# Values in fp32 on halves of the array's columns, distance table in fp32r

## The chip, the cores and the metric

One Trainium2 chip, one of its cores. The metric is the device time of one execution in microseconds (us), smaller is better. Before the change three runs took 2018.55 to 2023.57 us, with a median of 2019.44 us.

## The reference

Two transformer blocks on 512 frames with a width of 1024. The first has two attentions of eight heads of 64: one causal with a forgetting term (the "fox" heads), one in chunks with a table of biases by distance. The second adds 16 meta tokens in front and has an attention in a window of chunks with a sink (eight heads, keys and values shared by four), beside a gated linear attention. Around them stand projections, branch matrices, feed-forward parts and norms. The lines that the change touches, with softmax probabilities `p` that multiply values, and the table's bias:

```python
# first block, causal attention (q_block of 128 rows)
p = jax.nn.softmax(logits, axis=-1).astype(v.dtype)
return jnp.einsum('bhqk,bkhd->bqhd', p, v)
# first block, chunked attention
bias = rel_table[:, rel].astype(jnp.float32)
logits = jnp.einsum('bcqhd,bckhd->bchqk', qc, kb).astype(jnp.float32) * scale
logits = logits + bias[None, None]
p = jax.nn.softmax(logits, axis=-1).astype(v.dtype)
out = jnp.einsum('bchqk,bckhd->bcqhd', p, vb)
# second block, window attention
of = (jnp.einsum('bkgcqm,bmkd->bcqkgd', p[..., :N_META], vm)
      + jnp.einsum('bkgcqs,bcskd->bcqkgd', p[..., N_META:N_META + NB], vb))
```

## The kernel before

All is fp32 in and out. A large product is made of three matmuls in fp32r, a form of fp32 that is rounded: rounded times rounded, rounded times rest, rest times rounded. For that each weight and activation is split into a `_hi` tile (ScalarE, ACT, copies and rounds) and a `_lo` tile (VectorE, DVE, subtracts). Weights come in chunks of 1 MB into `W_raw`, and each chunk is split on ACT and DVE before its 48 matmuls.

The first attention stage (`front_steps`, with 64 units of 128 query rows of one head: eight fox heads, then eight chunked heads) is woven by a written table into the projections (`front_project`): in each step TensorE (PE) does nine to eleven projection matmuls and one unit's part. A unit goes this way. PE computes the scores of two heads at once in a PSUM bank each (`front_scores`, the two heads in the upper and lower 64 rows of the array), and adds the bias: for the chunked heads a plain fp32 matmul of the reversing matrix `exch` with the table `BAND`. DVE takes the maximum, ACT the exponential (tile `PR`), DVE the sum's inverse and the scaling. Two steps later PE turns the probabilities (L816) into the bank `TURNED`, ACT copies them out rounded (`PT_hi`), and DVE subtracts for the rest (`PT_lo`, L1962). After every fourth unit stands a phase (`front_values`): two heads, two blocks of 128 queries, the probabilities times the values. The stationary operand is `VHL`, a head's values rounded and their rest side by side, 128 columns; `PT_hi` and `PT_lo` stream through it one after the other. So the sum lies in two halves of the partitions of bank `PVOUT`, which ACT copies out (`OSIDE`) and DVE adds (`OSUM`, L1970); from two phases ACT and DVE make `O_hi` and `O_lo`. PE's queue waits before the next phase until DVE has added (`f_sum`), and before each turning until `PT_lo` of the unit before is done (`f_lo`).

The second attention stage (`win_steps`, 32 units) is woven in the same way into other projections. Its values are `VW`, its probabilities `PTW_hi`, `PTW_lo` for the window's keys and `PTM_hi`, `PTM_lo` for the 16 meta keys (`win_output`); the sums are `OSIDE2`, `OSUM2`, and the semaphores `att_lo`, `att_sum`.

The 24 MB of the conditioning matrix `wada` are mostly multiplied on DVE (L2584), three instructions for a part of the steps of the first stage. In the same stage DVE prepares the table (`band_bias`, L2006).

Of the kernel before, what the change touches and what calls it, by code (L numbers as in the profile page):

```python
# [9 lines left out]
FP32 = mybir.dt.float32  # L10
F32R = mybir.dt.float32r
# [5 lines left out]
P = 128  # L17
D = 1024
# [140 lines left out]
def build_program(nc, wts, wfg, wlow, wdown, wada, cond, vecs, xT, metaT, gate_w, band_rel, cf, cb, cw, cs, out):  # L159
    st, words = plan()  # L160
    n_chunks = len(words)
    with ExitStack() as ctx:
# [16 lines left out]
        with ExitStack() as over:  # L179
            PT_hi = sb("PT_hi", [P, 2, NB, 2 * P], F32R, over)  # L180
            PT_lo = sb("PT_lo", [P, 2, NB, 2 * P], F32R, over)
# [21 lines left out]
        OSIDE, OSUM = T[:, 2 * D:2 * D + SEQ], T[:, 2 * D + SEQ:2 * D + 2 * SEQ]  # L203
        OSIDE2, OSUM2 = T[:, 4 * TOK:4 * TOK + SEQ], T[:, 4 * TOK + SEQ:4 * TOK + 2 * SEQ]
# [15 lines left out]
        with ExitStack() as over:  # L220
            QH, QL, KH, KR, VHL = [], [], [], [], []
            for g in range(2):
# [4 lines left out]
                VHL.append(sb(f"VHL{g}", [P, NB, 4, P], F32R, over))  # L227
# [41 lines left out]
        with ExitStack() as over:  # L269
# [4 lines left out]
            VW = sb("VW", [P, NB + 1, 2, P], F32R, over)  # L274
            PTW_hi = sb("PTW_hi", [P, 2, SEQ], F32R, over)
            PTW_lo = sb("PTW_lo", [P, 2, SEQ], F32R, over)
            PTM_hi = sb("PTM_hi", [META, 2, 2 * P], F32R, over)
            PTM_lo = sb("PTM_lo", [META, 2, 2 * P], F32R, over)
# [378 lines left out]
        def _(pe):  # L657
# [95 lines left out]
            def front_scores(t):  # L753
# [13 lines left out]
                for o, n, _, _, _, _ in pair:  # L767
                    if fox:
                        last = mm(o[:, i * P:w], ident_b, causal_b, start=False, stop=True, skip_group_check=True)
                    else:  # L770
                        h = n - HEADS
# [2053 lines left out]
```

## Time and profile before

| | |
|---|---|
| median of three runs | 2019.44 us |
| the profiled execution | 2021.3 us |
| its span, first to last instruction | 2019.5 us |
| PE busy | 1956.0 us, 97% |
| DVE busy | 1023.5 us, 51% |
| ACT busy | 716.8 us, 35% |
| matmul records, weight loads | 10879 each |
| first attention stage | about 80 to 318 us |
| second attention stage | about 1296 to 1412 us |

How to read it: PE's row counts matmuls, PEld its weight loads, which run beside them. A matmul's shown length includes its way through the array, and the next one starts before it ends, so the distance between two starts tells what one costs. A plain fp32 matmul stands in the trace as two records, an fp32r matmul as one. The shape before the sizes is rows * columns of the stationary operand.

### The profile page before, as it was taken

Reading aid. Unit: us, or ns where it says so; the run is one execution under the profiler, and the core shown is the slowest. Engines: PE = TensorE matmul, PEld = TensorE weight load, DVE = VectorE, ACT = ScalarE, POOL = GpSimd, SP = SyncE. Lnnn points to the kernel's source line nnn. Section 1 sums busy time; section 2 is a strip of 40 time slices with the busy share of each in tenths; the row PEclk is TensorE's granted clock in tenths of the full one; section 3 lists DMA queues with packets and bytes.
Section 4 is the critical chain, followed back from the end, with each engine's and each line's share of the span. In section 5 each row is a group of like instructions: output and inputs, shape, how many; then the busy total and the mean of one; then the engine's idle time right before and its main releaser. Section 6 shows DMA issues by size and latency. Waiting matters only on the chain.

```text
span 2019.5 us, 26744 instructions
## 1 busy us (share of the span) xinstructions
PE 1956.0 (97%) x10879; PEld 1648.6 (82%) x10879; DVE 1023.5 (51%) x1428; ACT 716.8 (35%) x963; POOL 23.8 (1%) x45
## 2 busy tenths in 40 slices
PE   6999999998999999999999999999999999999998
PEld 2787888885888888689999999888878888888886
DVE  7688754447655543364344333776334454444323
ACT  3455444325544522252222222545223242222212
POOL 0100000000000000000000000000000000000000
PEclk8999999999999999989999999989999999999999
DMA  7644213221222222212222223210122222222221
GB/s 300 219 151 146 91 63 111 98 104 42 84 104 104 77 86 89 102 63 86 101 83 77 86 86 108 97 50 22 63 84 83 100 87 93 94 104 77 86 100 70
DMA packets 34848, 195.45 MB, mean 97 GB/s; under 512 B 3680, under 2 KB 3696, under 8 KB 19552
## 3 DMA queue, kind: packets, MB, share of 16 engines
q1 hardware_dynamic: 29008, 173.55, 24.4%
q0 software_dynamic: 5776, 21.02, 3.2%
q8 instruction: 43, 0.70, 0.1%
q14 instruction: 21, 0.17, 0.0%
HBM read 192.46 MB, written 2.10 MB: 96 GB/s over the span
## 4 chain that ended last, share of the span: by engine, by line
PE 91%; DVE 6%; ACT 1%; issue 1%; DMA 1%; DVEq 0%; ACTq 0%; SPq 0%
PE PS L659 90%; DVE W_lo L1865 1%; PE PS L816 1%; DMA ring<-in_wada 0%; DMA X<-in_xT 0%; DVE ring L2584 0%; ACT W_hi L1363 0%; DVE PT_lo L1962 0%; DVE stats L1947 0%; DVE X L2618 0%; DVE N L2418 0%; DVE A_low L2584 0%; DVE A_high L2584 0%; ACT T L1363 0%; DVE stats L2146 0%
## 5 line engine op out<-in xcount | busy, mean ns | idle before, releaser
L659 PE MATMUL PS<-H_hi,W_hi 128*128 128x512 f32 (+1 forms) x1944 | 616.0, 351 | 10.3 <-DVE H_lo L1873 3.8
L659 PE MATMUL PS<-H_hi,W_lo 128*128 128x512 f32 (+1 forms) x1944 | 618.6, 353 | 0.0
L659 PE MATMUL PS<-H_lo,W_hi 128*128 128x512 f32 (+1 forms) x1944 | 616.1, 351 | 0.0
L1865 DVE TENSOR_TENSOR W_lo<-W_raw,W_hi 128x2048 fp32r<-128x2048 f32 (+2 forms) x168 | 348.4, 2074 | 307.5 <-ACT W_hi L1363 307.2
L1363 ACT ACTIVATE W_hi<-W_raw 128x2048 fp32r<-128x2048 f32 (+2 forms) x168 | 291.8, 1737 | 373.6 <-PE PS L659 373.5
L659 PEld LDWEIGHTS PS<-H_hi,W_hi 128*128 128x128 f32 x1944 | 341.9, 190 | 64.3 <-issue 7.5
L659 PEld LDWEIGHTS PS<-H_lo,W_hi 128*128 128x128 f32 x1944 | 340.8, 189 | 48.5 <-issue 0.5
L659 PEld LDWEIGHTS PS<-H_hi,W_lo 128*128 128x128 f32 x1944 | 341.4, 190 | 47.6 <-issue 0.4
L659 PE MATMUL PS<-G_hi,W_lo 128*128 128x512 f32 (+1 forms) x704 | 210.7, 340 | 0.0
L659 PE MATMUL PS<-G_hi,W_hi 128*128 128x512 f32 (+1 forms) x704 | 210.4, 340 | 0.0
L659 PE MATMUL PS<-G_lo,W_hi 128*128 128x512 f32 (+1 forms) x704 | 210.2, 339 | 0.0
L2570 DVE TENSOR_TENSOR T<-PS,RS 128x528 f32<-128x528 f32 (+1 forms) x88 | 57.5, 694 | 174.0 <-PE PS L659 174.0
L659 PEld LDWEIGHTS PS<-G_lo,W_hi 128*128 128x128 f32 x704 | 120.9, 188 | 16.0
L659 PEld LDWEIGHTS PS<-G_hi,W_lo 128*128 128x128 f32 x704 | 120.7, 188 | 15.6
L659 PEld LDWEIGHTS PS<-G_hi,W_hi 128*128 128x128 f32 x704 | 120.5, 188 | 15.9 <-issue 0.4
L1363 ACT ACTIVATE G_hi<-T 128x1024 f32 (+3 forms) x33 | 35.3, 1071 | 230.0 <-DVE T L2576 208.9
L1363 ACT ACTIVATE T<-T 128x1024 f32<-128x1024 f32 (+1 forms) x38 | 40.6, 1068 | 196.9 <-DVE T L2570 149.4
L2542 DVE SCALAR_TENSOR_TENSOR T<-PS,V,T 128x511 f32<-128x511 f32 (+1 forms) x88 | 59.9, 743 | 55.8 <-ACT T L1363 55.8
L1363 ACT ACTIVATE PT_hi<-PS 128x128 fp32r<-128x128 f32 (+3 forms) x64 | 27.9, 436 | 103.4 <-PE PS L816 103.4
L659 PE MATMUL PS<-W_lo,H_hi 128*128 128x256 f32 x208 | 62.2, 299 | 0.0
L659 PE MATMUL PS<-W_hi,H_hi 128*128 128x256 f32 x208 | 59.7, 287 | 2.2 <-DVE W_lo L1865 2.1
L659 PE MATMUL PS<-W_hi,H_lo 128*128 128x256 f32 x208 | 59.6, 286 | 0.0
(323 smaller groups left out, 2071.1 us busy)
## 6 DMA issues: line engine op xcount, KB each, us to landing
W_raw<-in_wts SPq DMA_DIRECT2D x117, 1024.0 KB, 4.8
W_raw<-in_wdown SPq DMA_DIRECT2D x48, 704.0 KB, 4.0
ring<-in_wada POOLq DMA_DIRECT2D x32, 512.0 KB, 3.8
A_high<-in_wada SPq DMA_DIRECT2D x6, 1024.0 KB, 20.7
X<-in_xT SPq DMA_DIRECT2D x2, 1024.0 KB, 6.9
A_low<-in_wada SPq DMA_DIRECT2D x2, 1024.0 KB, 13.2
W_first<-in_wts SPq DMA_DIRECT2D x2, 1024.0 KB, 18.4
X<-in_xT POOLq DMA_DIRECT2D x1, 2048.0 KB, 9.0
```

What stands on the lines that cost most here:

```text
L659: return nc.tensor.matmul(*a, **kw)
L816: last = nc.tensor.transpose(PS[:, TURNED, j * P:(j + 1) * P], PR[:, u % 3, j * P:(j + 1) * P], ident)
L1363: return nc.scalar.activation(*a, **kw)
L1865: vector.tensor_tensor(W_lo[:, c.odd, 0:size], W_raw[:, c.odd, 0:size], W_hi[:, c.odd, 0:size].bitcast(FP32), ALU.subtract).then_inc(w_lo, 1)
L2542: ins = vector.scalar_tensor_tensor(out=tile[:, m, tap:SEQ], in0=PS[:, 4 * b.odd + 2 * m, 0:SEQ - tap], scalar=w, in1=tile[:, m, tap:SEQ], ...
L2570: ins = vector.tensor_tensor(halves((TA, TB)[k][:, m, 0:tok], tok), pview(b, m, tok), halves(RS[:, 0:tok], tok), ALU.mult)
```

## The change

The values of both stages are no longer split. ACT copies the turned probabilities whole (`PT`, `PTW`, `PTM`, fp32), and the values too (`VF`, `VW`, fp32, 64 columns a head); the subtractions on DVE go. In a phase each product is one plain fp32 matmul with 64 columns, the even head's on the left half of the array's columns and the odd head's on the right half, in turn. Their outputs lie in the upper and lower 64 partitions of `PVOUT`, complete, so `OSIDE` and `OSUM` go, and `O_hi`, `O_lo` are made from the bank. Two phases fill its two halves; a new pair waits for `O_lo` of the last (`f_olo`, `att_olo`). The table is split once into `BAND_hi` (ACT) and `BAND_lo` (DVE), `exch` is copied to fp32r, and a head's bias is two fp32r matmuls in place of one in fp32. The numbers of projection matmuls in a step stay.

```diff
             def front_scores(t):
-                        bias = BAND[:, h, P:2 * P] if i == 0 else BAND[:, h, :]
-                        last = mm(o[:, max(i - 1, 0) * P:w], exch, bias, start=False, stop=True, skip_group_check=True)
+                        for bias in (BAND_hi[:, h, c0:2 * P], BAND_lo[h // 4][:, h % 4, c0:2 * P]):
+                            last = mm(o[:, max(i - 1, 0) * P:w], EXCH[:, :], bias, start=False, stop=True, skip_group_check=True)
             def front_values(phase):
-                for half in range(2):
-                    for j in range(i0 + 2):
-                        c0 = max(j - i0, 0) * P
-                        for m, part in enumerate((PT_hi, PT_lo)):
-                            last = mm(PS[:, PVOUT, half * 2 * P + c0:(half + 1) * 2 * P], VHL[g][:, j, 2 * pair + half, :],
-                                      part[:, half, j, c0:2 * P], start=j == 0 and m == 0, stop=j == i0 + 1 and m == 1)
+                c = phase % 2 * 2 * P
+                for j in range(i0 + 2):
+                    c0 = max(j - i0, 0) * P
+                    for half in range(2):
+                        last = mm(PS[rows_of(half), PVOUT, c + c0:c + 2 * P], VF[g][:, j, 2 * pair + half, :], PT[:, half, j, c0:2 * P],
+                                  start=j == 0, stop=j == i0 + 1, skip_group_check=half == 1)
             def front_steps():   # PE; the same in win_steps
-                        pe.wait_ge(sem("f_lo"), v + 1)
+                        pe.wait_ge(sem("f_hi"), v + 1)
-                        if phase >= 1:
-                            pe.wait_ge(sem("f_sum"), 2 * phase)
+                        if phase >= 2 and phase % 2 == 0:
+                            pe.wait_ge(sem("f_olo"), phase // 2)
...
-                            pe.wait_ge(sem("f_lo"), u)
+                            pe.wait_ge(sem("f_hi"), u)
             def win_output(phase):
                 for half in range(2):
-                    o = PS[:, PVOUT, half * 2 * P:(half + 1) * 2 * P]
-                    for m, part in enumerate((PTM_hi, PTM_lo)):
-                        mm(o, VW[0:META, NB, half, :], part[:, half, :], start=m == 0, stop=False)
-                    values = win_values(phase)
-                    for n, (j, at, to, w) in enumerate(values):
-                        for m, part in enumerate((PTW_hi, PTW_lo)):
-                            last = mm(o[:, to:to + w], VW[:, j, half, :], part[:, half, at:at + w],
-                                      start=False, stop=n == len(values) - 1 and m == 1)
+                    mm(outs[half], VW[0:META, NB, half, :], PTM[:, half, :], start=True, stop=False, skip_group_check=half == 1)
+                values = win_values(phase)
+                for n, (j, at, to, w) in enumerate(values):
+                    for half in range(2):
+                        last = mm(outs[half][:, to:to + w], VW[:, j, half, :], PTW[:, half, at:at + w],
+                                  start=False, stop=n == len(values) - 1, skip_group_check=half == 1)
             def front_dense(s):   # ACT
+                    if k == LEAD + 4:
+                        activate(EXCH[:, :], exch, ACT.Copy)
+                        act.wait_ge(sem("band_bias"), 1)
+                        activate(BAND_hi[:, :, :], BAND, ACT.Copy).then_inc(sem("band_hi"), 1)
             def front_steps():   # DVE; the same in win_steps
-                        vector.tensor_tensor(PT_lo[part], PS[:, TURNED, 0:(i + 1) * P].rearrange("p (j q) -> p j q", q=P),
-                                             PT_hi[part].bitcast(FP32), ALU.subtract).then_inc(sem("f_lo"), 1)
...
-                            vector.tensor_tensor(OSUM[r, c], PS[r, PVOUT, half * 2 * P:(half + 1) * 2 * P], OSIDE[r, c], ALU.add
-                                                 ).then_inc(sem("f_sum"), 1)
             def front_dense(s):   # DVE
+                    if k == LEAD + 4:
+                        dve.wait_ge(sem("band_hi"), 1)
+                            vector.tensor_tensor(BAND_lo[g][:, :, :], BAND[:, h, :], BAND_hi[:, h, :].bitcast(FP32), ALU.subtract
+                                                 ).then_inc(sem("band_lo"), 1)
```

On PE, in the chunked heads' part of the first stage, a phase and the scores after it stand in this order before (the eight of the first head; the second head's eight read like them):

```order
723 L659 MATMUL PS<-PT_hi,VHL 128x256
724 L659 MATMUL PS<-PT_lo,VHL 128x256
725 L659 MATMUL PS<-PT_hi,VHL 128x256
726 L659 MATMUL PS<-PT_lo,VHL 128x256
727 L659 MATMUL PS<-PT_hi,VHL 128x256
728 L659 MATMUL PS<-PT_lo,VHL 128x256
729 L659 MATMUL PS<-PT_hi,VHL 128x128
730 L659 MATMUL PS<-PT_lo,VHL 128x128
```

The same phase of the changed kernel, with the scores and the bias that follow:

```order
660 L658 MATMUL PS<-PT,VF 64x256 x6
661 L658 MATMUL PS<-PT,VF 64x128 x2
662 L658 MATMUL PS<-KH,QH 128x256 x2
663 L658 MATMUL PS<-KH,QL 128x256 x2
664 L658 MATMUL PS<-KR,QH 128x256 x2
665 L658 MATMUL PS<-BAND_hi,EXCH 128x256
666 L658 MATMUL PS<-BAND_lo,EXCH 128x256
667 L658 MATMUL PS<-BAND_hi,EXCH 128x256
668 L658 MATMUL PS<-BAND_lo,EXCH 128x256
```

Sixteen value matmuls of 128 columns became eight of 64, and the bias of two heads, one plain matmul each before, became four.

On DVE, between two chunks' splits of the first stage, before:

```order
95 L1865 TENSOR_TENSOR W_lo<-W_raw,W_hi 128x2048 [waits w_hi]
96 L1947 TENSOR_REDUCE stats<-PS 128x1 [waits f_scores]
97 L1953 RECIPROCAL stats<-stats 128x1 [waits f_prob]
98 L1955 TENSOR_SCALAR PR<-PR,stats 128x512 [waits f_inverse]
99 L1962 TENSOR_TENSOR PT_lo<-PS,PT_hi 128x4x128 [waits f_hi]
```

The same place in the changed kernel:

```order
86 L1848 TENSOR_TENSOR W_lo<-W_raw,W_hi 128x2048 [waits w_hi]
87 L1930 TENSOR_REDUCE stats<-PS 128x1 [waits f_scores]
88 L1936 RECIPROCAL stats<-stats 128x1 [waits f_prob]
89 L1938 TENSOR_SCALAR PR<-PR,stats 128x512 [waits f_inverse]
90 L1960 SCALAR_TENSOR_TENSOR QL<-PS,QH 128x1024 [waits f_out_hi]
```

`PT_lo` is gone from each of the 64 units. Where the table is split, the changed kernel's DVE has this (BAND_lo once for heads 0 to 3 and once for 4 to 7):

```order
169 L2534 SCALAR_TENSOR_TENSOR ring,mod<-ring,silu_c 128x1024 [waits ada_loaded0]
170 L2002 TENSOR_TENSOR BAND_lo<-T,BAND_hi 128x1024 [waits band_hi]
171 L2002 TENSOR_TENSOR BAND_lo<-T,BAND_hi 128x1024
172 L1930 TENSOR_REDUCE stats<-PS 128x1 [waits f_scores]
173 L1936 RECIPROCAL stats<-stats 128x1 [waits f_prob]
174 L1938 TENSOR_SCALAR PR<-PR,stats 128x256 [waits f_inverse]
175 L1944 TENSOR_TENSOR O_lo<-PS,O_hi 128x512 [waits f_ohi]
176 L1848 TENSOR_TENSOR W_lo<-W_raw,W_hi 128x2048 [waits w_hi]
```

Nothing stood in the place of rows 170 and 171 before; the unit's statistics, `O_lo` and a weight chunk's rest queue behind them.

## Rows read from the trace of the kernel before

**Rows 1.** The page's busy times (part 1) and the chain by engine (part 4).
```profile
PE 1956.0 (97%) x10879; PEld 1648.6 (82%) x10879; DVE 1023.5 (51%) x1428; ACT 716.8 (35%) x963; POOL 23.8 (1%) x45
...
PE 91%; DVE 6%; ACT 1%; issue 1%; DMA 1%; DVEq 0%; ACTq 0%; SPq 0%
```

**Rows 2.** Busy time by stretch: us, PE, PEld, DVE, ACT, POOL, clock, DMA.
```profile
84.00:150.00 66.00, 62.27 (x411) 51.52 (x410) 54.84 (x120) 33.22 (x77) 7.56 (x13) 0.97 0.50 168
150.00:228.00 78.00, 72.99 (x467) 60.60 (x466) 65.17 (x134) 37.70 (x86) 6.11 (x11) 1.00 0.41 135
228.00:318.00 90.00, 90.00 (x540) 75.49 (x539) 55.24 (x121) 42.65 (x95) 1.34 (x2) 1.00 0.19 65
1296.00:1412.00 116.00, 105.93 (x821) 94.00 (x820) 80.96 (x267) 58.40 (x197) 0.00 (x0) 0.96 0.13 46
```

**Rows 3.** Timeline of PE, two first-attention phases: start us, us, engine, line, what.
```profile
153.58 0.28 PE L659 MATMUL PS<-PT_hi,VHL 128*128 128x256 f32 x1
...
154.55 0.50 PE L659 MATMUL PS<-KH,QH 64*128 64x512 f32 x2
...
226.79 0.29 PE L659 MATMUL PS<-PT_hi,VHL 128*128 128x256 f32 x1
...
227.39 0.28 PE L659 MATMUL PS<-PT_lo,VHL 128*128 128x256 f32 x1
...
228.70 0.39 PE L659 MATMUL PS<-KH,QH 64*128 64x256 f32 x2
```

**Rows 4.** Timeline of PE, two second-attention phases.
```profile
1355.42 0.38 PE L659 MATMUL PS<-PTM_hi,VW 16*128 16x256 f32 x1 [0.55 <-DVE PTM_lo L2171]
...
1357.92 0.48 PE L659 MATMUL PS<-KWH,WQH 64*128 64x272 f32 x2
...
1368.39 0.38 PE L659 MATMUL PS<-PTM_hi,VW 16*128 16x256 f32 x1
...
1370.46 0.39 PE L659 MATMUL PS<-KWH,WQH 64*128 64x272 f32 x2
```

**Rows 5.** Timeline of PE, the bias pair.
```profile
229.25 1.13 PE L659 MATMUL PS<-T,CF 128*128 128x256 f32 x4
230.22 0.27 PE L816 MATMUL PS<-CF,PR 128*128 128x128 f32 x1
```

**Rows 6.** Timeline of PE, fp32 matmuls on all columns, on 32 and on 64.
```profile
39.49 8.75 PE L659 MATMUL PS<-N,W_first 128*128 128x512 f32 x20
...
458.72 0.59 PE L659 MATMUL PS<-SQ,SW 128*32 128x512 f32 x1
...
459.15 0.59 PE L659 MATMUL PS<-SQ,SW 128*32 128x512 f32 x1
...
1419.01 3.40 PE L659 MATMUL PS<-LV,KL 16*64 16x128 f32 x64
```

**Rows 7.** Waits, 84 to 228 us, then 1296 to 1412: waiter, releaser, total us, times, longest.
```profile
PE PS L816 <- DVE PT_lo L1962: 4.6, 4, 1.2
...
PE PS L659 <- ACT PR L1363: 3.7, 4, 1.7
...
PE PS L1060 <- DVE PTM_lo L2171: 3.4, 5, 2.1
...
PE PS L659 <- ACT PRW L1363: 2.8, 2, 1.5
...
PE PS L659 <- DVE PTM_lo L2171: 2.0, 3, 0.9
```

**Rows 8.** Groups of VectorE by line: count, busy us, mean ns, idle before.
```profile
L1962 DVE TENSOR_TENSOR PT_lo<-PS,PT_hi 128x128 fp32r<-128x128 f32 (+3 forms) x64 | 31.2, 487 | 15.1 <-ACT PT_hi L1363 14.6
...
L2006 DVE TENSOR_TENSOR T<-T,BAND 128x2048 f32<-128x2048 f32 x1 | 2.3, 2291 | 0.0
```

**Rows 9.** Stretches at the lower clock, columns as in Rows 2.
```profile
1344.00:1347.60 3.60, 3.60 (x24) 3.20 (x23) 1.84 (x8) 1.16 (x5) 0.00 (x0) 0.56 0.00 0
...
1358.00:1361.50 3.50, 3.50 (x19) 3.11 (x20) 2.93 (x11) 1.60 (x7) 0.00 (x0) 0.51 0.46 145
```

More of the change, by code:

```diff
@@ L179, in build_program @@
         with ExitStack() as over:
-            PT_hi = sb("PT_hi", [P, 2, NB, 2 * P], F32R, over)
-            PT_lo = sb("PT_lo", [P, 2, NB, 2 * P], F32R, over)
+            PT = sb("PT", [P, 2, NB, 2 * P], FP32, over)
+            BAND_hi = sb("BAND_hi", [P, HEADS, 2 * P], F32R, over)
+            EXCH = sb("EXCH", [P, P], F32R, over)
         X = sb("X", [P, KT, TOK], FP32)
@@ L220, in build_program @@
         with ExitStack() as over:
[L221 removed]
+            QH, QL, KH, KR, VF, BAND_lo = [], [], [], [], [], []
             for g in range(2):
@@ L226, in build_program @@
                 KR.append(sb(f"KR{g}", [P, 2, SEQ], F32R, over))
-                VHL.append(sb(f"VHL{g}", [P, NB, 4, P], F32R, over))
+                VF.append(sb(f"VF{g}", [P, NB, 4, HEAD], FP32, over))
+                BAND_lo.append(sb(f"BAND_lo{g}", [P, HEADS // 2, 2 * P], F32R, over))
             with ExitStack() as first:
@@ L273, in build_program @@
             KWL = sb("KWL", [P, KEY_COLS], F32R, over)
[L274 to L278, printed above, removed]
+            VW = sb("VW", [P, NB + 1, 2, HEAD], FP32, over)
+            PTW = sb("PTW", [P, 2, SEQ], FP32, over)
+            PTM = sb("PTM", [META, 2, 2 * P], FP32, over)
+            sb("window_rest", [P, (NB + 1) * 2 * HEAD + 2 * SEQ + 4 * P], FP32, over)
             RESET = sb("RESET", [P, TOK], FP32, over)
@@ L1433, in front_steps @@
             def front_steps():
-                for t in range(UNITS + 6):
+                for t in range(UNITS + 5):
                     u = t - 2
@@ L1451, in front_steps @@
                                  accum_out=fstat[:, 1, t:t + 1]).then_inc(sem("f_prob"), 1)
-                    v = t - 3
-                    if 0 <= v < UNITS and v % NB == NB - 1:
-                        phase, c = v // NB, v // NB % 2 * 2 * P
-                        act.wait_ge(sem("f_pv"), phase + 1)
-                        if phase >= 2:
-                            act.wait_ge(sem("f_sum"), 2 * phase - 2)
-                        for half in range(2):
-                            ins = activate(OSIDE[rows_of(half), c:c + 2 * P],
-                                           PS[rows_of(1 - half), PVOUT, half * 2 * P:(half + 1) * 2 * P], ACT.Copy)
-                        ins.then_inc(sem("f_side"), 1)
-                    v = t - 5
+                    v = t - 4
                     if v >= 0 and v % (2 * NB) == 2 * NB - 1:
                         pair = v // (2 * NB)
-                        act.wait_ge(sem("f_sum"), 4 * pair + 4)
+                        act.wait_ge(sem("f_pv"), 2 * pair + 2)
                         if pair == ADA_PAIR:
                             act.wait_ge(sem("ada_used"), ADA)
-                        activate(O_hi[:, pair, :], OSUM, ACT.Copy).then_inc(sem("f_ohi"), 1)
+                        activate(O_hi[:, pair, :], PS[:, PVOUT, :], ACT.Copy).then_inc(sem("f_ohi"), 1)
                     yield
@@ L1554, in win_steps @@
             def win_steps():
-                for t in range(WIN_UNITS + 6):
+                for t in range(WIN_UNITS + 5):
                     if t == 1:
@@ L1577, in win_steps @@
                         activate(stat[:, 4, t:t + 1], vec("sinks", h), ACT.Exp, bias=stat[:, 0, t:t + 1]).then_inc(sem("att_sink"), 1)
-                    v = t - 3
-                    if 0 <= v < WIN_UNITS and v % NB == NB - 1:
-                        phase, c = v // NB, v // NB % 2 * 2 * P
-                        act.wait_ge(sem("att_pv"), phase + 1)
-                        if phase >= 2:
-                            act.wait_ge(sem("att_sum"), 2 * phase - 2)
-                        for half in range(2):
-                            ins = activate(OSIDE2[rows_of(half), c:c + 2 * P],
-                                           PS[rows_of(1 - half), PVOUT, half * 2 * P:(half + 1) * 2 * P], ACT.Copy)
-                        ins.then_inc(sem("att_side"), 1)
-                    v = t - 5
+                    v = t - 4
                     if v >= 0 and v % (2 * NB) == 2 * NB - 1:
                         pair = v // (2 * NB)
-                        act.wait_ge(sem("att_sum"), 4 * pair + 4)
-                        activate(O2A_hi[:, pair, :], OSUM2, ACT.Copy).then_inc(sem("att_ohi"), 1)
+                        act.wait_ge(sem("att_pv"), 2 * pair + 2)
+                        activate(O2A_hi[:, pair, :], PS[:, PVOUT, :], ACT.Copy).then_inc(sem("att_ohi"), 1)
                     yield
@@ L1941, in front_steps @@
             def front_steps():
-                for t in range(UNITS + 7):
+                for t in range(UNITS + 6):
                     if t < UNITS:
@@ L2134, in win_steps @@
             def win_steps():
-                for t in range(WIN_UNITS + 7):
+                for t in range(WIN_UNITS + 6):
                     if t == 2:
```

90 lines of the change are left out of this document (28 added, 62 removed).

## The prediction

> **What bounds the kernel now.** I read the busy times first and then the chain by engine: the reader is to see PE busy for 97% of the span and on 91% of the chain, with DVE at 6% [rows 1]. So what counts is what the change does to PE's queue: the time of its own matmuls, and the stretches in which it stands. The second view is the table by stretch, for the two stages that are touched. PE is not busy for 66.0 - 62.3 = 3.7 and 78.0 - 73.0 = 5.0 us in the first part of the first stage, for nothing in its last 90 us, and for 116.0 - 105.9 = 10.1 us in the second stage [rows 2]. DVE is busy for 83% of both stretches in which PE stands in the first stage. The third view, the waits, says for what PE stands: `PT_lo` 4.6 us and `PR` 3.7 in the first stage; `PTM_lo` 3.4 + 2.0 and `PRW` 2.8 in the second [rows 7]. The fourth is the timeline of PE, for what one matmul costs; the granted clock comes last.
>
> All sums are made against the profiled execution's 2021.3 us, which is 1.9 us above the median of the runs, 2019.4; I take the 1.9 off at the end.
>
> **The prices.** An fp32r matmul with 256 streamed columns takes 0.12 us: five starts from 226.79 to 227.39 [rows 3]. A plain fp32 one of 256 columns on the whole array takes half of the bias pair, (230.22 - 229.25) / 2 = 0.485 us [rows 5]. With 512 columns, the 20 records of 8.75 us have (8.75 - 0.59) / 19 = 0.43 us each, and a matmul is two records, so 0.86 us; 0.59 is the length of one record [rows 6]. The form that the change brings, two fp32 matmuls in turn on two parts of the array's columns, is in the trace in the norm's sums, on 32 columns each: a record of `SQ,SW` starts 0.43 us after the last, and in between lies one of its neighbour [rows 6]. So a pair of 512 columns, four records, takes 0.86 us, as much as one of them alone: the two run beside each other. For 256 columns I take half, 0.43 us for the pair. For 128 columns the loads could set the pace; `LV,KL`, fp32 of 128 columns on 64 by 64 parts, has 64 records in 3.40 us, at most 0.053 each, thus 0.21 for four records, and half of 0.43 is 0.215. I take 0.22.
>
> **The bias.** Twelve pairs of 256 columns go from 0.97 us to four fp32r at 0.12, 0.48: 12 x 0.49 = 5.9. Four pairs of 128 columns (the first block of each pair of heads) save half of that each, 1.0. Together -6.9 us.
>
> **The values of the first stage.** There are 16 phases. Eight with two key blocks took 154.55 - 153.58 = 0.97 us, eight with four took 228.70 - 226.79 = 1.91 [rows 3], 23.0 us in all. The former hold eight matmuls, four of 256 and four of 128 columns, 4 x 0.12 + 4 x 0.06 = 0.72; the 0.25 left over is what it costs to turn the array to another shape (the scores that follow use 64 rows). After: 0.43 + 0.22 = 0.65, and 3 x 0.43 + 0.22 = 1.51, with the same 0.25: 0.90 and 1.76. Saved: 8 x 0.07 + 8 x 0.15 = 1.8 us. Below this it could cost up to 0.2 us a phase, since the array changes shape at its start too: -1.8 to +1.4; I take -1.5, nearest to the counted matmuls.
>
> **The values of the second stage.** Four phases took 1370.46 - 1368.39 = 2.07 us, four 1357.92 - 1355.42 = 2.50 [rows 4]. The former hold eight matmuls of 256 columns and four of 128, 1.20 us; 0.87 us are over, for five changes of shape (into the 16 rows of the meta keys, out, in again, out, and to the scores), 0.17 each. After there are three changes, 0.52 us, and 0.43 + 0.43 + 0.22 = 1.08, in the longer ones 1.30: 1.60 and 1.82. Saved: 4 x 0.47 + 4 x 0.68 = 4.6 us. PE's own work in all: 6.9 + 1.5 + 4.6 = 13.0 us less.
>
> **The waits.** On DVE 64 subtractions of 0.487 us go in the first stage, 31.2 us of its busy time [rows 8], and with them the wait of each turning for `PT_lo`; the copies `OSIDE` and the additions go as well. So the waits of 4.6 us go, and of the 3.7 for `PR` all but the longest, 1.7, which stands ahead of the first phase: gross 6.6 us [rows 7]. What is late next is ACT's copy `PT`, which DVE waited on before, and in the 90 us in which PE never stood there is room for it. Added is the table's split: ACT's `BAND_hi` and DVE's `BAND_lo`, 2048 elements each, about the 2.3 us that DVE needs for such a tile in `band_bias` [rows 8]. Behind `BAND_lo` queue a unit's sum and scaling, for which PE waits before it turns; the 2.3 us stand against two `PT_lo` and two additions that went from the same steps, so I charge 1.0 us, between none and 2.3. The matmuls that need the table come 14 units or so later, and do not wait. Net -5.6 us, between -8.7 (all that PE stood) and 0. In the second stage 5.4 us of `PTM_lo` go, and about 1 of the `PRW` (the split of `VW` and the additions leave DVE's queue); against that, PE now waits for ACT's copy in some of these places. I take -5.4, between -10.1 and 0. After the last phase PE must wait for `O2A_lo` where it waited for the additions: one copy on ACT and one subtraction on DVE instead of two and two, started by the same matmul, so nothing.
>
> **The clock.** At two places of the second stage the granted clock is at 0.56 and 0.51 over 3.5 us, that is at its lower level of 1.2 GHz, and both stand behind stretches in which PE had stood for `PTM_lo`; half of such a stretch, 1.7 us, is lost [rows 9]. If PE stands less, some go. I take one, -1.7 us; the ends are +3.4 (two more) and -3.4.
>
> The sum: -6.9 - 1.5 - 4.6 - 5.6 - 5.4 - 1.7 = -25.7. Then 2021.3 - 25.7 = 1995.6, and by the median 1993.7 us. I predict **1994 us**. Since PE is the bound to the end, no later stage takes it back.
>
> The Trainium skill has a rule against this change ("TensorE: Matmul & The Clock Gate", Part 3, Packing small matmuls): a weight load overlaps with a matmul in flight only when its row group differs, and both halves here use all rows. By its figure of columns / 1.2 ns for a load, an estimate is 53 ns for 64 columns, for each record. The pair of the norm's sums has equal rows too, and there the two lie beside each other with no such gap.
>
> **The rivals.**
> - *The waits only move* (20%). PE's work falls by 13.0, but the chain of a unit (scores, maximum, exponential, scaling, turning, copy) comes due sooner and PE stands for `PR` and ACT's copies as long as it stood for `PT_lo`; the table costs its whole 2.3. For it: ACT's exponentials were waited on too [rows 7]. Against it: DVE loses a tenth of a stage's work or more. 2019.4 - 13.0 + 2.3 = 2008.7.
> - *The loads are not hidden* (5%). The value matmuls have 48 pairs in the first stage and 28 in the second, four records each, 304 loads. If each costs a slot such as a record of `LV,KL`, 0.05 us, that is 15 us: 1993.7 + 15 = 2009. Against it: 0.43 between two records of `SQ,SW` leaves no slot. This is the time that the skill's rule would give.
> - *The halves run one after the other* (6%), the slower side. A phase would be 2 x (0.485 + 0.25) + 0.25 = 1.72 and 2 x (3 x 0.485 + 0.25) + 0.25 = 3.66: 8 x (0.75 + 1.75) = +20. In the second stage 4 x 0.485 + 2 x 0.25 + 0.52 = 2.96 and 3.46: 4 x (0.89 + 0.96) = +7.4. With -6.9 for the bias and -11.0 for the waits, and nothing of the clock, +9.5: 2029. It is slower as soon as some three quarters of the overlap are missing. For it: with 128 rows and 64 columns the form is not in the trace; against it: 128 by 32 and 64 by 64 are, and both overlap.
> - *All of it goes* (10%): all waits that could go do (-3 more each stage) and both low stretches: about 1985.
>
> **How the numbers follow.** The forecast's own case has 59%. Its range, 1988 to 2001, has the waits' middle and the clock's. With the first rival and the better case the range is **1984 to 2010**; beyond it are the serial halves and tails. A measurement of this kernel tells 0.3%, 6 us, from no change. Faster by more (under 2013.4): the forecast, the better case and nearly all of the first two rivals, 0.88. Within: 0.06, their tails. Slower: the serial halves, 0.06.
>
> **What would show it.** Right: in the timeline of the changed kernel the phases of `PT,VF` take about 0.9 and 1.8 us to the next scores; the four `EXCH` matmuls 0.5; the second stage's phases 1.6 and 1.8; PE stands for less than 4 us from 84 to the end of the first stage and for less than 5 in the second. Wrong: phases over 1.7 and 3.5 us (serial); records of `PT,VF` spaced by more than 0.11 for 256 columns with both heads counted (0.43 for four), loads in between; rows of waits for `PT` or `PR` as long as those for `PT_lo` were; a low clock in the first stage where there was none.

## The result, and the profile after

The changed kernel takes 1986.9 us (median of 4 runs, 1985.1 to 1988.6), against 2019.7 for the kernel before in the same comparison (2018.6 to 2023.6). The ratio is 0.983, 95% interval 0.982 to 0.985: 32.8 us faster, where 25.7 were forecast. That lies within the stated range of 1984 to 2010, but 1.1 us below the narrower one, 1988 to 2001, which the forecast had for its own case. The profiled execution took 1988.6 us (its span 1986.8), 32.7 less than that of before; that is the difference the rows have to explain.

The page's busy times, and its chain by engine, answering to [rows 1]:

```profile
PE 1935.2 (97%) x10879; PEld 1620.8 (82%) x10879; DVE 956.7 (48%) x1248; ACT 698.5 (35%) x917; POOL 23.4 (1%) x45
...
PE 93%; DVE 4%; ACT 1%; issue 1%; DMA 1%; DVEq 0%; ACTq 0%
```

PE lost 20.8 us of busy time, so 11.9 us of the gain were time in which it stood. Its share of the chain rose by two points, and DVE's fell by two. The table by stretch, answering to [rows 2] (us, PE, PEld, DVE, ACT, POOL busy, clock, DMA share, GB/s; the last two stretches end with the shorter stages, the last one starting in the same place of the program):

```profile
84.00:150.00 66.00, 63.83 (x423) 50.88 (x422) 44.55 (x95) 30.69 (x72) 7.54 (x14) 0.97 0.52 177
150.00:228.00 78.00, 77.27 (x523) 61.61 (x522) 55.72 (x115) 38.48 (x86) 6.28 (x12) 1.00 0.41 135
228.00:313.00 85.00, 85.00 (x508) 67.45 (x507) 35.63 (x70) 39.63 (x77) 1.79 (x2) 1.00 0.25 88
1285.00:1378.00 93.00, 89.61 (x796) 78.30 (x795) 56.59 (x180) 49.53 (x178) 0.00 (x0) 1.00 0.16 57
```

From 84 to 228 us PE is not busy for 2.2 + 0.7 = 2.9 us instead of 8.7. In the second stage it is 3.4 instead of 10.1, and the clock there is 1.00 instead of 0.96. What PE still waits for, answering to [rows 7], from 84 to 228 us and then from 1270 to 1390:

```profile
PE PS L658 <- ACT PR L1363: 2.7, 2, 2.2
...
PE PS L658 <- ACT PRW L1363: 2.1, 2, 1.3
```

Every row for `PT_lo` and `PTM_lo` is gone. Left in the first stage is what the forecast left, one long wait for `PR`, now 2.2 us instead of 1.7; it stands at 87 us, before the second pair of scores. In the second stage `PRW` is left, and two short waits for ACT are new, this one and one of 0.23 us for `PTM` (below):

```profile
PE PS L658 <- ACT LV L1363: 0.5, 1, 0.5
```

To compare kernels I measure two lengths. The first stage goes from the first score matmul to the first of the merge `O_hi,W_hi`, the second from the first `KWH,WQH` to the first turning of `LL`. Rows of single tiles (count, ns min/median/max, first and last start in us) give both, here for the changed kernel:

```profile
L658 PE MATMUL PS<-KH,QH x64: 322/411/497, 80.5 to 289.3; 64*128 64x128 f32 x16, 64*128 64x256 f32 x16, 64*128 64x384 f32 x16, 64*128 64x512 f32 x16
...
L658 PE MATMUL PS<-O_hi,W_hi x64: 392/394/397, 317.1 to 394.6; 128*128 128x512 f32 x64
...
L658 PE MATMUL PS<-KWH,WQH x32: 330/389/395, 1285.5 to 1365.7; 64*128 64x272 f32 x24, 64*128 64x144 f32 x8
...
L1074 PE MATMUL PS<-CF,LL x10: 272/272/273, 1378.1 to 1379.1; 128*128 128x128 f32 x10
```

317.1 - 80.5 = 236.6 us, and 1378.1 - 1285.5 = 92.6. Before, the same rows give 250.3 and 112.7. So the stages gained 13.7 and 20.1 us; the rest of the program lost 1.1. The first length ends later than the 318 us given above for the stage, since the merge starts some projections after the last phase. In the table below "values" and "bias" are sums over their phases, each from its first start to the next matmul's.

| kernel | first stage | its values | bias | second stage | its values | median, us |
|---|---|---|---|---|---|---|
| before | 250.3 | 23.2 | 13.8 | 112.7 | 18.2 | 2019.7 |
| changed | 236.6 | 19.9 | 9.0 | 92.6 | 11.9 | 1986.9 |
| e1, first stage alone | 234.2 | 19.9 | 8.9 | 112.7 | 18.2 | 2005.0 |
| e2, second alone | 248.3 | 23.3 | 13.8 | 92.6 | 11.9 | 2001.9 |
| e3, old bias | 243.4 | 19.7 | 13.8 | 92.6 | 11.9 | 1991.8 |
| e4, head by head | 246.3 | 27.2 | 9.0 | 104.3 | 23.6 | 2004.2 |
| e5, rest back | 239.7 | 19.7 | 8.9 | 103.2 | 11.9 | 2002.5 |
| e6, one pass | 222.4 | 7.1 | 9.0 | 85.8 | 4.7 | 1968.6 |
| e7, sums back too | 247.6 | 19.7 | 8.9 | 106.6 | 11.9 | 2012.9 |
| e8, two by two | 234.8 | 20.3 | 9.0 | 92.6 | 11.9 | 1986.0 |

The phases themselves, on PE's timeline (start us, us, engine, line, what), answering to [rows 3, 4]. A short and a long one of the first stage, then two of the second:

```profile
99.76 0.40 PE L658 MATMUL PS<-H_lo,W_hi 128*128 128x512 f32 x1
100.09 0.87 PE L658 MATMUL PS<-PT,VF 128*64 128x256 f32 x8
100.89 0.50 PE L658 MATMUL PS<-KH,QH 64*128 64x512 f32 x2
...
191.49 1.73 PE L658 MATMUL PS<-PT,VF 128*64 128x256 f32 x16
193.15 0.39 PE L658 MATMUL PS<-KH,QH 64*128 64x256 f32 x2
...
1321.78 0.65 PE L658 MATMUL PS<-PTM,VW 16*64 16x256 f32 x4
1322.35 0.87 PE L658 MATMUL PS<-PTW,VW 128*64 128x256 f32 x8
1323.15 0.40 PE L658 MATMUL PS<-KWH,WQH 64*128 64x272 f32 x2
...
1332.16 0.65 PE L658 MATMUL PS<-PTM,VW 16*64 16x256 f32 x4 [0.23 <-ACT PTM L1363]
1332.74 1.09 PE L658 MATMUL PS<-PTW,VW 128*64 128x128 f32 x12
1333.76 0.39 PE L658 MATMUL PS<-KWH,WQH 64*128 64x272 f32 x2
```

They take 0.80, 1.66, 1.37 and 1.60 us where 0.90, 1.76, 1.60 and 1.82 were forecast. But such a sum leaves out what the phase does to the matmul ahead of it. That one, of 512 columns, starts 100.09 - 99.76 = 0.33 us before the phase, where before the change the distance is 0.24 (153.58 in [rows 3]):

```profile
153.34 0.40 PE L659 MATMUL PS<-H_lo,W_hi 128*128 128x512 f32 x1
```

The change to a 64-column shape at the start costs 0.09 to 0.10 us in each of the 16 phases, 1.5 us in all, and before the change it was not there. In the second stage the phases begin with a change (to 16 rows) in both kernels. The bias of two heads, on the same timeline, answering to [rows 5]:

```profile
226.14 0.39 PE L658 MATMUL PS<-BAND_hi,EXCH 128*128 128x256 f32 x1
226.37 0.28 PE L658 MATMUL PS<-BAND_lo,EXCH 128*128 128x256 f32 x1
226.49 0.28 PE L658 MATMUL PS<-BAND_hi,EXCH 128*128 128x256 f32 x1
226.60 0.28 PE L658 MATMUL PS<-BAND_lo,EXCH 128*128 128x256 f32 x1
226.72 0.38 PE L816 MATMUL PS<-CF,PR 128*128 128x128 f32 x2
```

It takes 0.58 us and not 0.48: the first of the four, the one that leaves the 64-row shape of the scores, is followed after 0.23 us, the others after 0.12.

The table's split on DVE, on its timeline:

```profile
171.76 2.36 DVE L2002 TENSOR_TENSOR BAND_lo<-T,BAND_hi 128x1024 fp32r<-128x1024 f32 x2
174.03 0.55 DVE L1930 TENSOR_REDUCE stats<-PS 128x1 f32<-128x384 f32 x1
```

It costs what was estimated. But PE is busy almost without a break in this place (16.91 of the 17 us from 161 to 178), so of the 1.0 us charged next to nothing shows. (One phase, at 178 us, takes 0.95 us instead of 0.80; in e3 below, without the split, none does, but none does in e5, with it, either.)

### The profile page after: what moved, and what is told of

Same layout as the page of the kernel before. It is cut to its first block, busy times and chain, and to the rows that moved or that the text cites. A ratio compares the mean times of both kernels' runs of the same rounds, so it can differ in the third digit from the quotient of the medians.

```text
span 1986.8 us, 26498 instructions
## 1 busy us (share of the span) xinstructions
PE 1935.2 (97%) x10879; PEld 1620.8 (82%) x10879; DVE 956.7 (48%) x1248; ACT 698.5 (35%) x917; POOL 23.4 (1%) x45
## 4 chain that ended last, share of the span: by engine, by line
PE 93%; DVE 4%; ACT 1%; issue 1%; DMA 1%; DVEq 0%; ACTq 0%
PE PS L658 92%; PE PS L816 1%; DVE ring L2534 1%; DMA ring<-in_wada 1%; DVE W_lo L1848 0%; DMA X<-in_xT 0%; DVE X L2568 0%; DVE N L2368 0%; DVE A_low L2534 0%; DVE A_high L2534 0%; ACT H_hi L1363 0%; DVE stats L1930 0%; DVE N L2473 0%; DVE H_lo L2454 0%; ACT W_hi L1363 0%
## 5 line engine op out<-in xcount | busy, mean ns | idle before, releaser
L1363 ACT ACTIVATE PT<-PS 128x128 f32<-128x128 f32 (+3 forms) x64 | 28.0, 438 | 105.1 <-PE PS L816 105.1
L1930 DVE TENSOR_REDUCE stats<-PS 128x1 f32<-128x128 f32 (+3 forms) x64 | 31.2, 488 | 67.7 <-PE PS L658 67.2
```

The lines of the kernel that those rows point to most:

```text
L1363: return nc.scalar.activation(*a, **kw)
L1930: vector.tensor_reduce(fstat[:, 0, t:t + 1], score_bank(t)[:, 0:w], AX.X, ALU.max, negate=True).then_inc(sem("f_max"), 1)
```

## The experiments

Eight kernels were run. The open questions were where the extra 7 us came from (in the second stage, by the table above), whether a shorter PE queue or a shorter chain of a unit brings the time, and why the pairs of halves cost what they do. The chain of a unit is what ACT and DVE do between PE's scores and its value matmuls.

The kernel before was run again beside them: 2020.0 us with e1 to e4, 2021.2 with e5 and e6, 2021.3 with e7 and e8, against 2019.7 beside the changed kernel. Where a difference to the changed kernel has a second number in brackets, that one compares the gains, each over its own run of before, which takes this shift out.

**e1 and e2, one stage each.** The edit is the change's own diff, for e1 only in the first attention and the table, for e2 only in the second:

```text
 e1:  front_values, front_scores, front_steps, VF, PT, BAND_hi, BAND_lo   as changed
      win_output, win_steps, VW, PTW, PTM                                 as before
 e2:  the other way round
```

> The change in the first stage alone (values and bias), the second stage as before. The changed kernel's first stage, from the first KH,QH matmul to the first of the branch matrix (O_hi,W_hi), is 236.6 us long and was 250.3. Theory (each stage gives its own part): this stage again about 237 us, the second (first KWH to the turning of LL) 112 to 113, the median 13 to 15 us under the kernel before, about 2006. Rival (the parts of the two stages help each other, for instance by what the clock does): under 8 us or over 20.

> The change in the second stage alone. It is 92.6 us long in the changed kernel and was 112.7, where 11.7 were forecast. Theory: it is as short here (92 to 94), no stretch at the lower clock in it, the median 18 to 20 us under the kernel before, about 2001. Rival (the three stretches at the lower clock come by where the stage falls in time, not by PE's waits): one or more such stretches stay, each 1.7 us, and the stage is 94 to 98 us long.

e1: 2005.0 us (2004.5 to 2006.4), ratio 0.992 [0.990, 0.994], 15.1 us less than the 2020.0 of before in this comparison. e2: 2001.9 (2000.3 to 2003.8), 0.991 [0.989, 0.992], 18.2 less. Together that is 33.3, so the two stages add up and don't disturb each other. e1 has the 112.7 us of before in the second stage, e2 the 92.6 of the changed kernel. The clock goes with the second stage's code. This is the stretch from 1325 to 1334 us in before, e1 and e2, inside that stage in all three:

```profile
1325.00:1334.00 9.00, 8.43 (x54) 7.21 (x53) 6.81 (x20) 4.39 (x13) 0.00 (x0) 0.82 0.23 72
```

```profile
1325.00:1334.00 9.00, 8.38 (x56) 7.50 (x58) 5.24 (x20) 3.30 (x13) 0.00 (x0) 0.81 0.01 2
```

```profile
1325.00:1334.00 9.00, 9.00 (x80) 8.11 (x80) 6.27 (x23) 4.61 (x19) 0.00 (x0) 1.00 0.33 117
```

Before has three low stretches of some 3.4 us in this stage, this one and the two of [rows 9]. They begin 32, 46 and 60 us after the stage's first matmul, and so do three in e1, though its stage starts 17 us earlier. In e2 and the changed kernel, where PE hardly stands, there is none. So they belong to the stage's own code, not to the time or to what ran before; e5 and e7 below, where one comes back with the waits, say that these have a part in it.

**e3, the old bias.** The table is not split, and a head's bias is one plain fp32 matmul:

```diff
-                        for bias in (BAND_hi[:, h, c0:2 * P], BAND_lo[h // 4][:, h % 4, c0:2 * P]):
-                            last = mm(..., EXCH[:, :], bias, ...)
+                        last = mm(o[:, max(i - 1, 0) * P:w], exch, BAND[:, h, c0:2 * P], start=False, stop=True, ...)
```

> The changed kernel with the bias of the chunked heads as before: one plain fp32 matmul of the reversing matrix with the whole table, no split of the table. Theory (PE's work counts one to one): 6.9 us of matmuls come back, 1.0 for the table's split goes, the first stage is 5 to 7 us longer than 236.6, the median about 1993. Rival (the trace's 13.8 us for the bias before and 9.0 after, counted from start to start, hold shape changes that stay): 4 to 5 us longer. Rival (other work hides it): under 2 us.

1991.8 us (1991.5 to 1994.0), ratio 0.985 [0.983, 0.987] to before, so 4.9 (4.5) more than the changed kernel. The bias takes its 13.8 us again instead of 9.0, one pair 0.97:

```profile
196.03 1.13 PE L658 MATMUL PS<-T,CF 128*128 128x256 f32 x4
197.00 0.27 PE L815 MATMUL PS<-CF,PR 128*128 128x128 f32 x1
```

The stage is 6.8 us longer, but 1.7 of it is a low-clock stretch early in it, which comes and goes between kernels with the same code there: the granted clock from 84 to 98 us is 0.88 before, after and in e7, 0.76 in e3 and e4, 1.00 in e1, in e2 (whose code there is that of before), in e5, e6 and e8. What is left, 5.1, is the bias with the table's split. The forecast had 6.9 less 1.0 for them: the first rival, changes of shape that stay, is borne out.

**e4, one head after the other.** The halves of the array are the same, but all matmuls of the even head come first:

```diff
-                for j in range(i0 + 2):
-                    c0 = max(j - i0, 0) * P
-                    for half in range(2):
+                for half in range(2):
+                    for j in range(i0 + 2):
+                        c0 = max(j - i0, 0) * P
                         last = mm(PS[rows_of(half), PVOUT, ...
```

and the same in `win_output`, the meta keys with their head.

> The changed kernel with a phase's matmuls in another order: first all of the head on the left half of the columns, then all of the head on the right half. The same matmuls and sizes. Theory (two heads' matmuls run beside each other only when they stand in turn): phases of the first stage of 1.7 and 3.6 us instead of 0.8 and 1.7, the first stage 20 us longer, the second 7 longer, the median 22 to 27 us over the changed kernel's, 2009 to 2014. Rival (the array overlaps them anyway, or the speed does not come from overlap): within 5 us of the changed kernel.

2004.2 us (2002.1 to 2008.5), 17.3 more than the changed kernel: ratio 0.991 [0.989, 0.993] to before, still faster. That is less than the 22 to 27 expected. The values of the second stage double (23.6 for 11.9), those of the first rise by 7.3 only (the stage by 9.7, of which 1.7 is the low-clock stretch that e3 has too). The timeline has a short phase, a long one, and one of the second stage:

```profile
102.66 0.88 PE L658 MATMUL PS<-PT,VF 128*64 128x256 f32 x8
103.47 0.50 PE L658 MATMUL PS<-KH,QH 64*128 64x512 f32 x2
...
196.77 2.65 PE L658 MATMUL PS<-PT,VF 128*64 128x256 f32 x16
199.35 0.39 PE L658 MATMUL PS<-KH,QH 64*128 64x256 f32 x2
...
1333.91 0.64 PE L658 MATMUL PS<-PTM,VW 16*64 16x256 f32 x2
1334.48 0.86 PE L658 MATMUL PS<-PTW,VW 128*64 128x256 f32 x4
1335.28 0.64 PE L658 MATMUL PS<-PTM,VW 16*64 16x256 f32 x2
1335.85 0.86 PE L658 MATMUL PS<-PTW,VW 128*64 128x256 f32 x4
1336.64 0.40 PE L658 MATMUL PS<-KWH,WQH 64*128 64x272 f32 x2
```

The short phase takes 0.81 us, as in turn: in the trace the odd head's first record starts at 102.676 us, 0.013 after the even head's first, though four records stand ahead of it. In the long phase (2.58 us instead of 1.66) it starts at 197.689, with the even head's fifth of eight (197.683). So in these phases PE starts matmuls of one half ahead of up to four queued records of the other half, and not of eight. In the second stage two changes of the row shape lie between the heads, and nothing overlaps: 2.73 us instead of 1.37. My expectation of fully serial halves in the first stage was wrong by this.

**e5, the rest back.** The subtractions are made again (their results are not used), and PE waits for them as before:

```diff
-                        pe.wait_ge(sem("f_hi"), v + 1)
+                        pe.wait_ge(sem("f_lo"), v + 1)
...
+                        dve.wait_ge(sem("f_hi"), u + 1)
+                        vector.tensor_tensor(T[...], PS[:, TURNED, ...], PT[...], ALU.subtract).then_inc(sem("f_lo"), 1)
```

and the same in the second stage, with two subtractions into `window_rest`.

> The changed kernel with DVE's subtractions put back, into a tile that nobody reads, and with PE waiting for them as before (before each turning and each phase). PE's matmuls are those of the changed kernel. It prices the waits alone. Theory (forecast): +5.6 us in the first stage (236.6 to 242) and +5.4 in the second (92.6 to 98), with stretches at the lower clock back in the second; the median 11 to 17 us over the changed kernel's. Rival A (the gain of the second stage beyond forecast, 20.1 against 11.7, is the wait chain and the clock that hangs on it): the second stage gets 10 to 15 us longer, the three low stretches are back. Rival B (it is PE's work, mis-sized): it gets under 5 us longer.

2002.5 us (2002.1 to 2003.4), ratio 0.991 [0.989, 0.993] to its before (2021.2), 15.5 (14.1) more than the changed kernel, within what was expected. Its table of the second stage, and PE's longest waits there:

```profile
1288.00:1391.00 103.00, 93.40 (x791) 79.27 (x790) 72.23 (x243) 50.30 (x178) 0.00 (x0) 0.98 0.14 51
```

```profile
PE PS L658 <- DVE window_rest L2144: 3.0, 4, 1.5
PE PS L1060 <- DVE window_rest L2144: 2.0, 6, 0.7
```

PE is not busy for 9.6 us instead of 3.4, yet the stage is 10.6 longer, 1.7 of it one low-clock stretch, where rival A had expected three. In the first stage it is only +3.1 us instead of 5.6, or 4.8 when the early low-clock stretch is left out, which the changed kernel has and e5 has not.

**e7, the sums back too.** As e5, and also the copies to the side and the additions, with PE, ACT and DVE waiting for them:

```diff
+                            ins = activate(T[rows_of(half), ...], PS[rows_of(1 - half), PVOUT, c:c + 2 * P], ACT.Copy)
...
+                            vector.tensor_tensor(T[r, ...], PS[r, PVOUT, c:c + 2 * P], T[r, ...], ALU.add).then_inc(sem("f_sum"), 1)
...
+                        if phase >= 1:
+                            pe.wait_ge(sem("f_sum"), 2 * phase)
```

> The run with the subtractions put back (e5_rest_back), and beside them, after each phase, ACT's two copies of 64 x 256, DVE's two additions and PE's wait for them before the next phase, as before the change; nobody reads the results. PE's matmuls stay those of the changed kernel. With it the whole of the old chain on ACT and DVE is back. Theory (the gain is PE's work plus this chain, nothing else): the first stage 236.6 + (13.7 less the 3.4 of the values' matmuls and the 4.9 of the bias) = 242, the second 92.6 + 20.1 - 6.3 = 106.4, three stretches at the lower clock in it, the median 2008 to 2010. Rival (the additions are hidden, and the rest came from somewhere else): both stages within 1 us of the run without the additions, 239.7 and 103.2, the median 2002.

2012.9 us (2011.7 to 2014.4), ratio 0.996 [0.994, 0.997] to its before (2021.3): 26.0 (24.4) more than the changed kernel and just outside what was expected. This kernel has PE's new work and nearly the old chain. PE's longest waits from 84 to 228 us are:

```profile
PE PS L818 <- DVE T L1968: 5.8, 5, 1.3
PE PS L658 <- ACT PR L1367: 3.8, 4, 1.8
PE PS L658 <- DVE T L1968: 2.5, 2, 1.5
```

12.1 us, against the 8.7 that PE stood there before [rows 2]. PE has less to do, and stands longer for the same chain. Its work in the first stage is 4.9 (bias) + 3.4 (values) - 1.5 (the changes of shape at the phases' starts) = 6.8 us shorter than before, the stage only 2.7. So the expectation of 242 us for this stage, which took the matmuls' part and the chain's to add up, was wrong: it is 247.6. Taking the chain away is worth 11.0 us once the matmuls are short, and the shorter matmuls are worth 2.7 as long as the chain is there.

The second stage is 106.6 us, against 106.4 expected, but that is partly luck: one low-clock stretch came back and not three. Against before, the stage is 6.1 us shorter, of which 3.4 are the two low stretches fewer; so of the 6.3 us of shorter matmuls 2.7 arrive here too. The chain, with the clock that hangs on it, is worth 14.0 us here, which is this stage's gain beyond the 6.3 of the matmuls.

**e6, one pass.** Probabilities and values in bf16 in the same number and places; it leaves precision out, and serves to ask what PE's time is worth once the chain is short:

```diff
-            PT = sb("PT", [P, 2, NB, 2 * P], FP32, over)
+            PT = sb("PT", [P, 4, NB, 2 * P], BF16, over)
```

and `VF`, `VW`, `PTW`, `PTM` alike.

> The changed kernel with probabilities and values rounded to bf16 by the same copies, so that each value product is one pass of one record in place of fp32's four passes in two; it leaves out all of their precision below bf16. Everything else as it is. Theory (PE's work counts one to one, no wait behind it): of 0.65 us of streaming in a short phase and 1.51 in a long one 3/4 goes, 8 x 0.49 + 8 x 1.13 = 13 us, and 4 x 0.81 + 4 x 0.98 = 7 us in the second stage: the median 17 to 20 us under the changed kernel's. Rival (the unit's chain over DVE and ACT becomes the bound once PE's part shrinks): under 12 us, with new waits for PR, PT or PRW.

1968.6 us (1968.3 to 1970.7), ratio 0.974 [0.973, 0.976] to before, 18.3 (19.8) less than the changed kernel. The long phase falls to a third:

```profile
185.94 0.57 PE L658 MATMUL PS<-PT,VF 128*64 128x256 bf16 x8
186.45 0.39 PE L658 MATMUL PS<-KH,QH 64*128 64x256 f32 x2
```

The values take 12.8 + 7.2 = 20.0 us less. The stages are 14.2 us shorter, of which 1.7 is the early low-clock stretch, and 6.9, together 19.4: with the short chain nine tenths or more of PE's saved time arrive. With the old chain, in both stages of e7, it was two fifths.

**e8, two by two.** Two matmuls of one head, then two of the other, to test what e4 suggested:

```diff
-                for j in range(i0 + 2):
-                    c0 = max(j - i0, 0) * P
-                    for half in range(2):
+                for half, j in [(half, j) for j0 in range(0, i0 + 2, 2) for half in range(2) for j in (j0, j0 + 1)]:
+                        c0 = max(j - i0, 0) * P
```

> The changed kernel with the first stage's phases in the order: two key blocks of the left head, two of the right, and so again. In the run with a head after the other the short phases (two key blocks) lost nothing, and in the long ones the right head's first record started with the left head's fifth. Theory (PE issues to the other half of the columns up to four records ahead): the long phases take 1.66 us as in turn, the first stage is 236.6 us long within 1.5, the median within 4 us of the changed kernel's 1987. Rival (each change from one half to the other after more than one matmul costs): long phases of 1.9 to 2.3 us, the stage 2 to 5 us longer.

1986.0 us (1984.8 to 1986.8), ratio 0.982 [0.981, 0.984] to before: not to be told from the changed kernel (0.982 to 0.985). The first stage is 1.8 us shorter than there, outside the 1.5 allowed for, but 1.7 of that is the early low-clock stretch, which e8 has not. A long phase takes 1.72 us against 1.66 in turn and 2.58 head by head:

```profile
189.11 1.78 PE L658 MATMUL PS<-PT,VF 128*64 128x256 f32 x16
190.83 0.39 PE L658 MATMUL PS<-KH,QH 64*128 64x256 f32 x2
```

Four records of the same half in a row cost next to nothing; eight do.

## Why the prediction was right, and where it was off

The mechanism held, and so did the stated range, though only by the room that its better case had given it: 1986.9 lies under the 1988 of the forecast's own case. The sum was 7 us short. In the first stage it came out by luck (14.0 forecast, 13.7 measured), since a bias too large stood against waits too small; in the second it was 8.4 us short. Term by term, of the profiled execution:

| term | forecast | measured | from |
|---|---|---|---|
| bias | -6.9 | -4.9 | table; e3 |
| values, first stage | -1.5 | -1.9 | -3.4 in the table, +1.5 at the phases' starts |
| waits, first stage | -5.6 | about -6.9 | 13.7 less the two above |
| values, second stage | -4.6 | -6.3 | table; e4 |
| waits, second stage | -5.4 | about -8.7 | 20.1 less 6.3 and 5.1 |
| clock, second stage | -1.7 | about -5.1 | three stretches gone; e1, e2 |
| the rest | 0 | +1.1 | spans |

*The bias* is the smaller by the change of shape. I had counted it for the values, but took the four fp32r matmuls at their steady 0.12. The old plain matmuls had the same change inside their 0.97 (two of 256 columns at half of 0.86 make 0.86), and there too it was not told apart. A pair then saves 0.39 us and not 0.49; twelve are 4.7 us, so of the 1.0 us for the four pairs of 128 columns next to nothing came.

*The values* of the first stage saved 1.9 us, near the forecast and within its bounds. Less is left over inside a phase beside the counted matmuls, 0.80 - 0.65 = 0.15 and 1.66 - 1.51 = 0.15 instead of 0.25, and the change of shape at the start, which the forecast had named as a risk of up to 0.2 us, costs 0.1. The price of a pair, taken from `SQ,SW` of [rows 6], was right. In the second stage 1.37 - 1.08 = 0.29 is left over instead of 0.52, so 6.3 us were saved and not 4.6. A change of shape costs less here than I had read from the old phases, but which part of those was something else was not tried.

*The waits* are the step that was mis-sized, with the clock. I took the rows of waits as their price, 5.4 us in the second stage. PE's time not busy fell by 6.7, and the stage without the matmuls' share and the clock by 8.7. The difference is one of reading. An fp32r record lasts 0.28 us while the next starts 0.12 after it [rows 3], so the first 0.16 us of a wait can lie under a record still in flight, and no row has them. Two turnings of the kernel before show it:

```profile
1352.52 0.28 PE L659 MATMUL PS<-W_hi,H_hi 128*128 128x256 f32 x1
1352.92 0.30 PE L1060 MATMUL PS<-CF,PRW 128*128 128x128 f32 x1
...
1366.05 0.28 PE L659 MATMUL PS<-W_hi,H_hi 128*128 128x256 f32 x1
1366.53 0.30 PE L1060 MATMUL PS<-CF,PRW 128*128 128x128 f32 x1 [0.20 <-DVE PTM_lo L2171]
```

Without a wait the next matmul would start after 0.12 us. In the second place it starts after 0.48, so 0.36 us are lost where the row has 0.20; in the first after 0.40, so 0.28 are lost where the timeline shows no wait at all. I measured each wait of the second stage in this way, as the distance between two starts less that of the same pair without a wait. The sum is 12.3 us before, where the rows show 10.1, and 3.9 in the changed kernel, where they show 3.4: 8.4 less, which is all but 0.3 of the 8.7. In e5 it is 12.4 (9.6 shown). In e7 it is 15.6 (12.6 shown), with one low stretch where before has three; a PE slowed by its clock may wait less, which was not tried.

In the first stage it is the same on a smaller scale: PE's time not busy fell by 5.8 us, the cost of the waits by about 6.9. There the wait for `PR` shrank by 1.0 and not by the 2.0 forecast, and the 1.0 us charged for the table's split was not lost. The marks set for this held: under 4 and under 5 us not busy, 2.9 and 3.4 measured.

*The clock.* I counted on one stretch of three, since I had found two and priced one; all three went. By e1 and e2 they belong to the code of their stage, and by e5 and e7 its waits have a part in them, but the sum of these does not give their number: three with 10.1 us not busy before, one with 9.6 in e5, one with 12.3 in e7. Which wait starts one was not tried.

*The rivals.* "The waits only move" (20%, 2008.7) is refuted: ACT's copies `PTM` and `LV`, 0.23 and 0.5 us once each, are the only new releasers in the rows, and the longest wait for `PR` grew from 1.7 to 2.2 us and no further. But e7 shows how near it was: had the rests and sums stayed, the same shorter matmuls would have brought 8.4 us and not 32.8. "The loads are not hidden" is refuted: the records of 256 columns in a long phase start in pairs 0.216 us apart, the two of a pair 0.007 us apart; over all 16 it is one every 1.66 / 16 = 0.104 us. The phase has 0.15 us beside its counted 1.51, and a slot of 0.05 for each record would add 0.8. With it falls, for two column halves with the same rows, the rule that the prediction quoted from the Trainium skill ("TensorE: Matmul & The Clock Gate", Part 3, Packing small matmuls). The rows of before spoke against it already: PEld is busy for 82% of the span beside PE's 97% [rows 1], so loads overlapped with matmuls in flight where nearly all have the full 128 rows. "The halves run one after the other" is refuted in the changed order and came out for the second stage in e4's, at 2.73 us for a phase against the 2.96 worked out. The nearest in size was "all of it goes" (10%, 1985): in the second stage that is what happened, with all three low stretches. It was given too little for its place between the bounds I had written down myself, -10.1 for the waits and -3.4 for the clock (with three stretches instead of the two I had found, -5.1).

What stays open: e7 splits the table and makes `O_hi` from the bank, so it is not the old chain to the letter, and its 2.7 us in the first stage bound only roughly what the matmuls alone would bring. No kernel has the old matmuls with the short chain, so what the chain alone is worth was not measured. The 1.1 us that the rest of the program lost (1.0 before rounding) are spread over it: 0.3 before the first stage, 0.4 between the stages and 0.2 behind them. Low-clock stretches between them don't explain it, for from 440 to 900 us the granted clock is 0.98 before and 0.99 in the changed kernel. What started the early stretch near 88 us, which comes and goes with the same code, stays open too.

## What to carry to other kernels

On a kernel that is bound by one engine, shortening that engine's work and shortening the chain that feeds it belong together: here the shorter matmuls alone brought 2.7 us of the first stage, with nearly the old chain, and both together 13.7. When you price waits, take the rows of waits as a lower bound, compare distances between starts with and without a wait, and count all the low-clock stretches of the stage, which may go with its waits. When you price matmuls, count each change of the array's shape, also the one ahead of the first matmul, for the new kind as for the old, and put two column halves in turn or at most four records apart, with no change of rows between them.

## What the runs showed of the hardware

- Plain fp32 matmuls on two column halves of 64 with the same 128 rows run beside each other: eight records in 0.80 us, the change to the next shape included, and 16 in 1.66, in pairs whose two start 0.007 us apart. Pair follows pair after 0.216 us, half of the 0.43 us that a record of 512 columns takes alone on the whole array.
- PE started a matmul of one column half 0.013 us after one of the other half, with four records of that other half queued between them (e4), but not across a change from 16 to 128 rows. With eight queued between them, it started with the fifth (e4's long phase).
- The first fp32r matmul of 256 columns after scores on 64 rows takes 0.23 us to the next start instead of 0.12, and the last one of 512 columns before values on 64 columns 0.33 instead of 0.24, so such a change costs about 0.1 us.
- Low-clock stretches of 3.4 us, 1.7 us lost in each, stood three times in a stage of 113 us in which PE was not busy for 10 us in all (no single wait over 2.1), once where it was 9.6 over 103 (e5) or 12.3 over 106 (e7), and never where it was 3.4 over 93.
